# Level products of a gated linear attention as three bfloat16 passes instead of one float32 pass, in a two-block Trainium2 kernel

## The reference, cut to what matters

```python
def hgrn2_chunkwise(q, k, log_f, v):
    ...
    def step(state, chunk):
        qc, kc, lfc, vc = chunk
        cum = jnp.cumsum(lfc, axis=2)
        o_inter = jnp.einsum('bhtk,bhkv->bhtv', qc * jnp.exp(cum), state)
        rel = cum[:, :, :, None, :] - cum[:, :, None, :, :]
        decay = jnp.where(causal[:, :, None], jnp.exp(jnp.minimum(rel, 0.0)), 0.0)
        scores = jnp.einsum('bhtsk,bhsk->bhts', qc[:, :, :, None, :] * decay, kc)
        o_intra = jnp.einsum('bhts,bhsv->bhtv', scores, vc)
        ...
```

## Time and profile before

| what | us |
|---|---|
| median of 3 runs | 3046.41 (3042.95 to 3048.2) |
| span of the profiled execution | 3044.6 |
| PE busy | 2860.1 (94%) |
| DVE busy | 1953.3 (64%) |
| ACT busy | 1323.3 (43%) |
| POOL busy | 1280.0 (42%) |

### The profile page before, as it was taken

One profiled execution on the slowest core, in us unless ns is written; L12 is line 12 of the kernel. 1 busy time (PEld: TensorE's weight loads), 2 busy tenths in 40 slices (PEclk: granted clock), 3 DMA queues, 4 the chain that ended last, 5 costly groups with the idle time before them and its releaser, 6 DMA issues.

```text
span 3044.6 us, 49166 instructions
## 1 busy us (share of the span) xinstructions
PE 2860.1 (94%) x19746; PEld 1749.1 (57%) x19746; DVE 1953.3 (64%) x3140; ACT 1323.3 (43%) x2341; POOL 1280.0 (42%) x1060
## 2 busy tenths in 40 slices
PE   7889998999979988999999999999999999999998
PEld 3438776874429667864466565664764444444443
DVE  3785997763589996644875665666663654444445
ACT  3353654652366646643344554454543322122222
POOL 1302482010602580012545846767661635555551
PEclk9999999999989999999999999999999999999999
DMA  8223241002201340021101111201122201111111
GB/s 292 110 70 122 84 154 52 12 22 104 94 14 43 125 139 29 12 87 59 67 29 42 70 42 42 70 31 66 43 85 110 70 28 56 56 56 44 54 44 74
DMA packets 50898, 213.45 MB, mean 70 GB/s; under 512 B 4680, under 2 KB 9968, under 8 KB 34032
## 3 DMA queue, kind: packets, MB, share of 16 engines
q1 hardware_dynamic: 42288, 195.63, 18.5%
q10 hardware_dynamic: 8384, 14.68, 1.4%
HBM read 190.36 MB, written 19.94 MB: 69 GB/s over the span
## 4 chain that ended last, share of the span: by engine, by line
PE 41%; DVE 3%; POOL 3%; ACT 2%; issue 1%; DMA 0%; ACTq 0%; POOLq 0%; DVEq 0%
PE big L284 7%; PE big L286 7%; PE big L285 7%; PE banks L284 4%; PE banks L286 4%; PE banks L285 4%; PE banks L1183 3%; POOL w_lo L596 2%; PE banks L1162 0%; PE banks L1153 0%; PE banks L1134 0%; PE banks L1164 0%; PE banks L1170 0%; DVE arena L2567 0%; DVE arena L2568 0%
## 5 line engine op out<-in xcount | busy, mean ns | idle before, releaser
L653 POOL TENSOR_TENSOR w_lo<-stage,w_hi 128x512 bf16<-128x512 f32 x340 | 429.7, 1295 | 367.3 <-ACT w_hi L1390 367.0
L646 POOL CAST w_hi<-stage 128x512 bf16<-128x512 f32 x252 | 179.6, 753 | 781.4 <-PE big L286 588.5
L284 PE MATMUL big<-w_hi,ht_hi 128*128 128x256 bf16 (+2 forms) x1280 | 358.0, 288 | 22.7 <-DVE arena L1913 4.7
L596 POOL TENSOR_TENSOR w_lo<-stage,w_hi 128x512 bf16<-128x512 f32 x174 | 249.6, 1445 | 263.6 <-ACT w_hi L1590 263.6
L285 PE MATMUL big<-w_lo,ht_hi 128*128 128x256 bf16 (+2 forms) x1280 | 357.9, 288 | 0.0
L286 PE MATMUL big<-w_hi,ht_lo 128*128 128x256 bf16 (+2 forms) x1280 | 357.8, 287 | 0.0
L284 PE MATMUL big<-ht_hi,w_hi 128*128 128x512 bf16 x816 | 310.2, 380 | 24.7 <-POOL w_lo L596 8.7
L286 PE MATMUL big<-ht_hi,w_lo 128*128 128x512 bf16 x816 | 310.0, 380 | 0.0
L285 PE MATMUL big<-ht_lo,w_hi 128*128 128x512 bf16 x816 | 309.8, 380 | 0.0
L284 PE MATMUL big<-arena,w_hi 128*128 128x512 bf16 (+1 forms) x716 | 222.5, 328 | 21.4 <-DVE arena L2154 8.4
L285 PE MATMUL big<-arena,w_hi 128*128 128x512 bf16 (+1 forms) x716 | 222.6, 328 | 0.0
(11 more groups left out here) (395 smaller groups left out, 7144.2 us busy)
## 6 DMA issues: line engine op xcount, KB each, us to landing
stage<-in_w SPq DMA_DIRECT2D x130, 1024.0 KB, 4.8
arena<-in_w_ada SPq DMA_DIRECT2D x48, 512.0 KB, 4.4
arena<-in_x SPq DMA_DIRECT2D x16, 512.0 KB, 9.2
xs<-arena SPq DMA_DIRECT2D x16, 512.0 KB, 2.6
arena<-xs SPq DMA_DIRECT2D x16, 512.0 KB, 7.2
gt<-arena ACTq DMA_DIRECT2D x16, 256.0 KB, 2.5
arena<-gt ACTq DMA_DIRECT2D x16, 256.0 KB, 2.6
out_x<-arena SPq DMA_DIRECT2D x8, 512.0 KB, 2.6
```

Source lines behind the costliest of these rows:

```text
L284: pe.matmul(out, ah, bh, start=start, stop=False, skip_group_check=onto)
L596: return pool.tensor_tensor(lo, x, hi, ALU.subtract)
L646: pool.tensor_copy(w_flat[0][:, w0 + c0:w0 + c1], stage[:, n % RAW_RING, c0:c1]).then_inc(s_w_hi_split, mark(s_w_hi_split, n, q))
L653: ins = pool.tensor_tensor(w_flat[1][:, w0 + c0:w0 + c1], stage[:, n % RAW_RING, c0:c1], w_flat[0][:, w0 + c0:w0 + c1], ALU.subtract)
```

## The change

The level products are made of split operands. `level_high` (ScalarE) writes the high parts of queries and keys as bfloat16, `level_low` (VectorE) the low parts, value less high part. At level 0 all keys (1024 elements a partition) and the second-block queries (512) are split, in two instructions on either engine. At levels 1 to 6 one instruction on either engine covers the first-block keys and the second-block queries together, 2 x 512 elements: the only ones that have changed and are used. The parts lie in areas of their own (`LEVEL_AT`: head 0 where the states and outputs come later, head 1 where TH lies). TensorE calls `mm3` for each tile, 24 products of 64 columns a level, and waits for `level_lo`.

```diff
@@ TensorE
-                        if st:
-                            pe.wait_ge(s_hgrn_dve, when(s_hgrn_dve, "lvl", b, c, st - 1))
-                        else:
-                            pe.wait_ge(s_hgrn_dve, when(s_hgrn_dve, "qf", b, c))
+                        pe.wait_ge(s_level_lo, when(s_level_lo, b, c, st))
                         g = take(pe, "t", "hs", *key)
+                        nj = 64 // h
                         for s in range(NT):
-                            q = QE[c][:, s * P:(s + 1) * P].rearrange("p (j two h) -> p j two h", two=2, h=h)[:, :, 1, :]
-                            ins = pe.matmul(g[:, s * 64:(s + 1) * 64].rearrange("p (j h) -> p j h", h=h), KF[c][:, s * P:(s + 1) * P], q, start=True, stop=True)
+                            ins = mm3(pe, g[:, s * 64:(s + 1) * 64].rearrange("p (j h) -> p j h", h=h), [level_keys(c, i)[:, s * P:(s + 1) * P] for i in range(2)],
+                                      [level_queries(c, i, h)[:, s * nj:(s + 1) * nj, :] for i in range(2)], True, True)
@@ ScalarE
+                def level_high(c, st):
+                    if st:
+                        act.wait_ge(s_hgrn_dve, when(s_hgrn_dve, "lvl", b, c, st - 1))
+                        act.wait_ge(s_hgrn, when(s_hgrn, b, c, st - 1))
+                        act.activation(level_part(c, 0, 1 << st), level_raw(c, 1 << st), ACT.Copy).then_inc(s_level_hi, mark(s_level_hi, b, c, st))
+                    else:
+                        act.wait_ge(s_hgrn_dve, when(s_hgrn_dve, "qf", b, c))
+                        act.activation(level_keys(c, 0), KF[c], ACT.Copy)
+                        act.activation(level_queries(c, 0, 1), QE[c].rearrange("p (j two h) -> p j two h", two=2, h=1)[:, :, 1, :], ACT.Copy).then_inc(s_level_hi, mark(s_level_hi, b, c, 0))
...
                 def hgrn(c, st):
                     key = (b, c, st)
+                    if st == "diag":
+                        if c == 0 and b:
+                            act.wait_ge(s_hgrn_dve, when(s_hgrn_dve, "og", b - 1, 1))
+                        if c:
+                            act.wait_ge(s_rg_dve, when(s_rg_dve, "one_a2", b, 1))
+                        level_high(c, 0)
+                    if isinstance(st, int) and st < 6:
+                        level_high(c, st + 1)
...
                         tanh_r(b, 0)
+                    hgrn(*hsteps[4 + 2 * n])
...
                     act.activation(R_[n], R_[n], ACT.Exp, scale=NSP8[:, 2 * b + n:2 * b + n + 1]).then_inc(s_rg_act, mark(s_rg_act, "a", b, n))
+                    hgrn(*hsteps[5 + 2 * n])
@@ VectorE
+                def level_low(c, st):
+                    dve.wait_ge(s_level_hi, when(s_level_hi, b, c, st))
+                    if st:
+                        dve.tensor_tensor(level_part(c, 1, 1 << st), level_raw(c, 1 << st), level_part(c, 0, 1 << st), ALU.subtract).then_inc(s_level_lo, mark(s_level_lo, b, c, st))
+                    else:
+                        dve.tensor_tensor(level_keys(c, 1), KF[c], level_keys(c, 0), ALU.subtract)
+                        dve.tensor_tensor(level_queries(c, 1, 1), QE[c].rearrange("p (j two h) -> p j two h", two=2, h=1)[:, :, 1, :], level_queries(c, 0, 1), ALU.subtract).then_inc(s_level_lo, mark(s_level_lo, b, c, 0))
```

24 lines of the change are left out of this document (21 added, 3 removed).

## The result

The changed kernel takes 3083.69 us (median of 4 runs, 3080.05 to 3086.64) against 3046.61 (4 runs, 3042.95 to 3048.2) for the kernel before, run beside it: a ratio of 1.0125, 95% interval 1.0111 to 1.014. It is 37 us slower. The prediction had the sign, but only +11.7 us, and its range ended at 3080. The profiled execution of the changed kernel spans 3084.9 us. Of the executions behind the times of this document one, of quiet_after, took 7168 us and is not compared.

The account below looks back on a forecast made before the run. TensorE was taken to set the pace: 59 us saved, 68 given back by the split chain, +8.7; clock dips +3.0; together +11.7 on 3044.6, plus 1.8 to the median, gives 3058.1 us, range 3030 to 3080.

Parts of the forecast that it names:

- Part 1: Level products on TensorE: 24 bfloat16 products take 0.68 us a step instead of 1.73, saving 59 us over 56 steps.
- the rule cited in part 1: Weight load on TensorE takes columns / 1.2 ns, 107 ns for 128; a step would take 2.57 us, losing 47 us.
- Part 2: Splits at each level: ScalarE conversions of 1.04 us, 62 in all; VectorE subtractions of about 1.35, 81 in all.
- Part 3: Chain through VectorE and ScalarE between level steps, 4.5 to 6.5 us: 68 us given back, +8.7 net.
- The test that the prediction set: Pair 1, from the start of level 3 to the start of ga: 14.8 us before, 16.0 after.
- they collide more: VectorE and GpSimd: every multiplication in levels 0 to 3 takes 1.64 us, +24 to +40, 3080; chance 0.14.
- they collide less: VectorE and GpSimd: multiplications at 0.68, copies at 0.7, subtractions at 1.23 us; -12, giving 3034; chance 0.19.
- The strided reading: Strided query columns in TensorE's level products double a product's price to some 55 ns: +12, 3070; chance 0.07.
- the slow weight load: Level products on TensorE load weights no faster in bfloat16, 108 ns a record, 2.6 us a step: 3118; chance 0.03.
- the fully hidden waits: All of TensorE's waits at the levels are hidden and the 59 us stay saved: 2989; chance 0.07.
- The rule cited from the Trainium skill: VectorE tensor_tensor with both inputs in SBUF and a reading GpSimd instruction exclude each other; subtractions take 1.52 us and above.
- The clock: Granted clock dips after new stalls ahead of levels 6 and 0, one counted a pair at even chances: +3.0 us.

Follow-up runs that it names:

- quiet_after: The changed kernel with GpSimd's low parts and sums of block 2's seven-product chunk weights made over 8 of 512 columns: 3010.0 us, ratio 0.9875.
- busy_waits: The changed kernel with 48, 66 and 36 idle products filling TensorE's three longest waits (level 0 of both heads, level 6 of head 0): 3082.56 us.
- vector_splits: The changed kernel with the high parts also made on VectorE, right ahead of the low parts, and none on ScalarE: 3098.08 us, ratio 1.0175.
- split_once: The changed kernel without the splits of levels 1 to 6, which read the parts made at level 0: 3032.79 us, ratio 0.9963 against the kernel before.
- p5_first: The changed kernel with ScalarE's copy of p5 moved ahead of the conversion for the next level: 3088.52 us, ratio 1.0145.

## Why the prediction was right and wrong

**Part 1 was right.** A step starts at 1635.17 and the next product at 1635.88: 0.71 us, against 0.68. The strided columns cost next to nothing: the products of a step start 29.1 to 30.6 ns apart where the granted clock is 1.00, at every level. The outcome by the rule cited in part 1, 2.57 us a step, is refuted by the same rows. Saved: 59 us, as forecast. The prediction named a step of over 1 us as a sign of being wrong, and 8 of the 56 took 1.12 to 1.27, seven of them at level 0. That is the clock and not the products: in busy_waits, with the clock at 1.00, the same level 0 of head 0, pair 1, takes 0.73 us instead of 1.25.

**Part 2 was right on the means, wrong on the instruction that mattered.** ScalarE's part took 1.07 (1.04 taken), VectorE's 1.30 (1.35 taken). Level 0's two were put at 2.0 together; they took 1.26 + 1.72 = 2.98. The second was priced by its width at 0.7, as when GpSimd is quiet, though by its shape it is a multiplication, for which the earlier trace rows gave 1.64 as well.

**Part 3 had the right shape and the wrong sizes; it is the step that failed.** The chain of VectorE and ScalarE in head 1 was put at 4.5 us, under TensorE's 5.21, and took 5.6 to 6.6; in head 0 the prices of VectorE's instructions were too low in the same way. Lateness in us of head 0, pair 1, and head 1, pair 0, against before, with the stage's own start taken off ("end" is the transpose, which follows level 6's step by a few products); for levels 4 and 5 of head 1 the forecast figures are read off its words "winning 1.05 a step".

| | L0 | L1 | L2 | L3 | L4 | L5 | L6 | end |
|---|---|---|---|---|---|---|---|---|
| head 0 forecast | 2.1 | 2.7 | 2.4 | 2.7 | 2.9 | 3.2 | 5.0 | 3.9 |
| head 0 measured | 3.2 | 4.8 | 5.3 | 5.3 | 6.1 | 6.2 | 8.1 | 8.7 |
| head 1 forecast | 3.6 | 3.6 | 3.3 | 3.0 | 2.0 | 1.0 | 0 | -1.2 |
| head 1 measured | 4.5 | 4.4 | 4.6 | 3.9 | 3.4 | 3.7 | 3.0 | 2.0 |

- Head 0 loses 1.1 us at level 0 (the narrow low part), 1.0 at level 1 (total 1.64 instead of 1.0, second multiplication 1.64 instead of 1.2, less small gains; the prediction's own terms for this level add up to 1754.3 and not to its 1753.9, so that it was 0.4 too early even by its prices), 0.8 at level 2 (both multiplications at 1.75), of which 0.3 come back at level 3, 0.6 at level 4 (ScalarE behind sigmoid and tanh), and 1.7 between level 6's step and the transpose, where the granted clock was 0.85 and 0.73. The test that the prediction set, from level 3 to the start of ga, came out near it, 16.5 us against 16.0 (14.8 before), since most of the loss lies ahead of level 3.
- Head 1 was to run at TensorE's pace from level 3 on, with a chain of 4.5 us. The chain took 5.6 to 6.6 in the rows above: a total of 64 columns took 1.00 and the next ones 0.67 and 0.53 instead of some 0.2, one of the two multiplications 1.64 to 1.75 at each of levels 3 to 5, one low part 2.10, and ScalarE left VectorE idle for 0.5 each time. The prediction had named this test ("a chain below 5.2 us", "none ahead of levels 4 to 6"), and it came out against it.
- The errors are 4.8 us in head 0 of pair 1 and 3.2 in head 1 of pair 0. If each pair has both, less in head 0 of pair 0 (+4.3 against +1.6 forecast), that is 3 x 8.0 + 2.7 + 3.2 = 30 us. With the forecast's +8.7 it gives 39, and the span grew by 40.3. The forecast for pair 0 rested on GpSimd being idle in its v. It isn't: the narrow low part took 1.69 there too, and the multiplications of level 1 took 1.75 and 1.76.

What was wrong in method: the averages of the earlier trace rows were taken for the price of a multiplication, and the dear price given only where a row had shown it. The mean of L2612 hardly moved (972 ns for 947), and L2613's was 1013. But the mean mixes 0.68 and 1.64, and a chain that is just too long at the dear price loses each time, while at the cheap one TensorE's pace hides the gain. Before, the levels had 2 us of slack that took up the dear ones. The change used that slack up: 27 of the 112 multiplications took over 1 us before and 35 do now, so that it is less their number that changed than what one of them costs.

**The rivals.** What happened is nearest to the rival "they collide more", put at 3080 and a chance of 0.14; its price for it, 24 to 40 us, covers the 30 found. Its condition, 1.64 for every multiplication in levels 0 to 3, was met by 26 of 64 only; dear totals, narrow low parts and multiplications at levels 4 to 6 made up for the rest. The forecast's reason for staying below it, a mean of 0.95, was the mistake. The rival "they collide less" (-12) is what quiet_after shows in a kernel where GpSimd's work is left out: -8.0 by the spans, -4.8 by the medians. The strided reading, the slow weight load and the fully hidden waits are excluded by the product rows and the 72.5 us of waits. (The last one's 2989 should be 2987 by its own terms, 3046.4 - 59.)

How often they collide, and who pays, can be counted in the changed kernel's trace. Two low parts of head 1, pair 0, with GpSimd's rows beside them:

```profile
1639.64 1.23 DVE L2571 TENSOR_TENSOR arena<-arena 128x1024 bf16<-128x1024 f32 x1 [0.50 <-ACT arena L1749]
1639.68 2.32 POOL L630 TENSOR_TENSOR stage<-stage 128x512 f32<-128x512 f32 x1
...
1645.20 1.16 POOL L616 TENSOR_TENSOR w_lo<-arena,w_hi 128x512 bf16<-128x512 f32 x1
1645.34 2.10 DVE L2571 TENSOR_TENSOR arena<-arena 128x1024 bf16<-128x1024 f32 x1 [0.48 <-ACT arena L1749]
```

The first started 0.04 us ahead of GpSimd's instruction and took its usual time; GpSimd's took 2.32 us, where it takes 1.27 with VectorE idle. The second started 0.14 us behind GpSimd's, which took its usual 1.16, and ended 1.08 us after it. So the one that starts second pays, and this sorts all cases:

- Of the 112 multiplications 35 took 1.10 to 1.76 us. At the start of each a GpSimd instruction had 0.55 to 1.21 us left, and each ended 0.55 us after it. The other 77 took 0.68; 10 of them overlap GpSimd for 79% or more, and there GpSimd's started with them or after (within 0.01 us of each other, either can be the one that pays).
- All 8 narrow low parts (L2574) started in the middle of a GpSimd instruction, took 1.68 to 1.79 and ended 0.59 us after it.
- Of the 48 low parts of 1024 elements (L2571) 37 hardly overlap GpSimd and took 1.22 or 1.23. Of the other 11, the 7 that started first took the same, and the 4 that started second took 2.09 or 2.10.

The rule cited from the Trainium skill, "SBUF — State Buffer", section Who interferes with whom, holds in all these cases, with the 0.68 and 1.64 as its numbers. What the prediction made of it for the low parts, 1.52 and above, did not come true: 44 of the 48 took 1.22 or 1.23, because most don't meet GpSimd and in 7 cases GpSimd was the one shut out. It left out who starts first.

**The clock.** Put at +3.0. The profile shows 18 us more of it. The dip behind level 6 of head 0 alone costs 1.3 to 1.7 us a pair, as filling that wait shows, 6.3 in all, over twice the forecast. Filling the three waits gave back at most 5 in the end, because the levels that came earlier met GpSimd more often.

Open: the 9 us of TensorE's busy time that neither level products nor clock explain, and how the 37 us split between ScalarE's queue and VectorE in ri, since only both together were varied there (vector_splits moved one and loaded the other).

## What to carry to other kernels

Before moving work into an engine's slack, take the slack at the dear price of each instruction, not at its mean: if a line has two prices (here 0.68 and 1.64 us, by whether a GpSimd instruction is under way when it starts), the chain must fit at the dear one, or the saving on the busy engine can come back as its waits, as here. Splitting an operand anew at each step of a recurrence puts two engines and a handover in series between the steps; where the parts were made once a head (split_once, whose scores are wrong) the same products paid, by 0.4%. A wait seen at one instruction may be worth nothing to remove if another releaser stands close behind it (p5_first). And a few us won in one place can be lost to new collisions further on (busy_waits), so read the levels behind the repaired one too.
